# Bias rows stored from 128 partitions, head norms in finer turns, and two preparations moved into the turns of other products

## The reference

```python
# first block: differential attention, then a norm for each head
ob = diff_attention(q1, q2, k1, k2, vh, lam, slopes)
ob = rms_norm(ob, g_subln) * (1.0 - lam_init)
# second block
hm = mlstm_chunkwise(mq, mk, mv, i_gate, log_f)
hm = hm * lax.rsqrt(jnp.mean(hm * hm, axis=-1, keepdims=True) + NORM_EPS)
y_ml = jax.nn.sigmoid(mo) * (hm * mlstm_norm)
x = x + rms_norm_2(jnp.concatenate([y_nsa, y_ml], axis=-1) @ w_out, mix_norm_post)
h = rms_norm_2(x, xattn_norm_pre)
mem_n = rms_norm_2(mem, mem_norm)
q = (h @ w_xq) * XATTN_HEAD_DIM ** -0.5
k, v = jnp.split(mem_n @ w_xkv, 2, axis=-1)
p = jax.nn.softmax(jnp.einsum('bshd,bmhd->bhsm', q, k), axis=-1)
x = x + rms_norm_2(jnp.einsum('bhsm,bmhd->bshd', p, v).reshape(B, S, D_MODEL) @ w_xo, xattn_norm_post)
```

## Time and profile before

| | us |
|---|---|
| median of 3 runs | 2117.9 |
| lowest and highest | 2117.48, 2119.8 |
| the profiled execution | 2119.19 |
| its span in the trace | 2117.4 |
| TensorE busy in the span | 1821.1 |
| DVE busy | 742.0 |
| ACT busy | 641.0 |
| POOL busy | 169.1 |

### The profile page before, as it was taken

How to read it: one execution, slowest core, us unless ns; L and a number is a source line. 1 busy time by engine, 2 the same in 40 slices (tenths; PEclk the granted TensorE clock), 3 DMA queues, 4 the chain that set the end, 5 groups by cost and what they waited for, 6 DMA issues and landing times.

```text
span 2117.4 us, 21821 instructions
## 1 busy us (share of the span) xinstructions
PE 1821.1 (86%) x8908; PEld 1276.2 (60%) x8908; DVE 742.0 (35%) x1540; ACT 641.0 (30%) x1077; POOL 169.1 (8%) x134
## 2 busy tenths in 40 slices
PE   7969999997898887888489777997889879999998
PEld 4848656786333333333167555765678758888887
DVE  4245344455111111211432355544463452222323
ACT  4224455423011000100331245454342342222223
POOL 0000001130111111110000000001000100000111
PEclk9979889998899999989789688997999989999999
DMA  7541100248699999999722110111232112322311
GB/s 210 76 141 65 55 20 21 73 180 310 253 397 417 415 408 398 412 407 411 281 75 84 41 58 18 41 60 69 98 123 80 50 40 96 113 80 80 119 60 40
DMA packets 78434, 337.57 MB, mean 159 GB/s; under 512 B 7883, under 2 KB 15691, under 8 KB 65400
## 3 DMA queue, kind: packets, MB, share of 16 engines
q1 hardware_dynamic: 73208, 327.70, 41.4%
q0 software_dynamic: 5120, 8.40, 1.2%
HBM read 327.69 MB, written 16.78 MB: 163 GB/s over the span
## 4 chain that ended last, share of the span: by engine, by line
PE 48%; DMA 18%; DVE 8%; ACT 5%; issue 2%; POOL 0%; SPq 0%; DVEq 0%; POOLq 0%; ACTq 0%
PE ps L500 47%; DMA otf<-in_w 17%; DVE splitr L565 1%; ACT splitr L576 1%; ACT arenaf L2637 1%; PE ps L2500 1%; ACT hr L771 1%; DVE arenaf L2585 1%; DVE xf L2893 1%; DVE tq L797 0%; DVE hr L805 0%; DMA arenaf<-yd 0%; DVE xf L2099 0%; DVE arenaf L2603 0%; DVE otf L2432 0%
## 5 line engine op out<-in xcount | busy, mean ns | idle before, releaser
L500 PE MATMUL ps<-hr,splitr 128*128 128x512 f32 x2400 | 586.3, 404 | 14.3 <-POOL hr L848 9.8
L500 PEld LDWEIGHTS ps<-hr,splitr 128*128 128x128 f32 x2400 | 464.1, 196 | 116.1 <-POOL hr L848 12.1
L500 PE MATMUL ps<-splitr,hr 128*128 128x512 f32 (+2 forms) x1584 | 291.4, 346 | 28.1 <-ACT arenaf L726 23.1
L500 PEld LDWEIGHTS ps<-splitr,hr 128*128 128x128 f32 x1584 | 253.4, 197 | 62.3 <-ACT arenaf L726 23.3
L565 DVE TENSOR_TENSOR splitr<-ring,splitr 128x2048 fp32r<-128x2048 f32 x63 | 146.8, 2333 | 237.7 <-ACT splitr L576 237.6
L500 PE MATMUL ps<-ring,arenaf 128*64 128x512 f32 x352 | 176.9, 661 | 21.8 <-DMA ring<-in_w 21.8
L576 ACT CAST splitr<-ring 128x2048 fp32r<-128x2048 f32 x63 | 119.7, 1903 | 188.4 <-PE ps L500 162.0
L500 PE MATMUL ps<-arenaf 128*64 128x128 f32 (+11 forms) x898 | 134.8, 364 | 27.2 <-DVE arenaf L1684 8.7
L1848 DVE TENSOR_TENSOR arenaf<-arenaf,ps 64x512 f32<-64x512 f32 x32 | 21.8, 681 | 329.0 <-ACT arenaf L1843 329.0
L565 DVE TENSOR_TENSOR splitr<-arenaf,splitr 128x2048 fp32r<-128x2048 f32 x29 | 69.5, 2396 | 139.7 <-ACT splitr L576 139.7
L1843 ACT ACTIVATE arenaf<-ps 64x512 f32<-64x512 f32 x32 | 19.0, 594 | 326.4 <-PE ps L500 326.4
(11 more groups left out here) (342 smaller groups left out, 2001.7 us busy)
## 6 DMA issues: line engine op xcount, KB each, us to landing
ring<-in_w SPq DMA_DIRECT2D x22, 2048.0 KB, 35.6
arenaf<-in_w SPq DMA_DIRECT2D x22, 2048.0 KB, 40.5
splitf<-in_w SPq DMA_DIRECT2D x21, 2048.0 KB, 35.3
hf<-in_w SPq DMA_DIRECT2D x20, 2048.0 KB, 36.0
ring<-in_w_in SPq DMA_DIRECT2D x11, 2048.0 KB, 10.9
otf<-in_w SPq DMA_DIRECT2D x11, 2048.0 KB, 39.6
ring<-in_w_gate_up SPq DMA_DIRECT2D x6, 2048.0 KB, 7.8
arenaf<-in_w_in SPq DMA_DIRECT2D x4, 2048.0 KB, 21.1
```

The lines of the kernel that those rows point to most:

```text
L500: return te.matmul(out, lhsT, rhs, start=start, stop=stop)
```

## The change

- The biases are repeated 16 times on DVE (`rlx`, 33x128), so TensorE's product gives each row in 16 partitions; `vr` is now 128x1024 in `junk`, and the store writes 8 copies from each of 128 partitions. The waits for the store move from step 5 of the differential attention (DVE and ACT) to DVE's start of fox.
- DVE's part of `spread` becomes a task of its own, `table`, a turn ahead of TensorE's. `ML_SIDE` and `ML_LAST` are laid out anew, with one step of a head norm in a turn.
- `pe_T` and `walk_T` call `tick` for each token tile of each piece. The cross weights get the group of `wout`, so their first piece follows `wout1`'s last.
- In steps 12 to 15 of `xa` the first four rows of outputs are split; behind it the other four.

```diff
-            dense(f"xkv{c}", "w_xkv_2", 512 * c, 512, mode="FFTT"[c], group="x")
+            dense(f"xkv{c}", "w_xkv_2", 512 * c, 512, mode="FFTT"[c], group="m")
...
-            dense(f"xq{c}", "w_xq_2", 512 * c, 512, group="x")
+            dense(f"xq{c}", "w_xq_2", 512 * c, 512, group="m")
...
-        vr = OT[0:8, 1536:2560]
+        vr, rlx = junk[:, 1024:2048], OT[0:33, 1536:1664]
...
-                    if i == 0 and len(names) > 1:
                         tick()
-                for t in range(nt):
-                    tick()
...
                     lead(p)
-                    if i == 0 and len(jobs[job]) > 1:
+                    for t in range(nt):
+                        if i == len(jobs[job]) - 1:
+                            done(t)
                         tick()
-                for t in range(nt):
-                    done(t)
-                    tick()
...
-                elif what == "spread":
+                elif what == "table":
...
-                sp.dma_start(io["vd"], vr.rearrange("h (o n) -> h o n", o=1).broadcast_to([8, 128, 1024])).then_inc(
+                sp.dma_start(io["vd"].rearrange("h (a e) n -> (h a) e n", e=8),
+                             vr.rearrange("p (o n) -> p o n", o=1).broadcast_to([128, 8, 1024])).then_inc(
...
-                    mm(ps[0:8, :], rl, oh[:, 512 * half:512 * half + 512], True, True).then_inc(
+                    mm(ps[:, :], rlx, oh[:, 512 * half:512 * half + 512], True, True).then_inc(
...
                     if t == 2:
+                        for w in ve_at(("rl",)):
+                            ve.wait_ge(*w)
+                        ve.tensor_copy(thirds(rlx, 8), rl.rearrange("p (h o) -> p h o", o=1)
+                                       .broadcast_to([33, 8, 16])).then_inc(*ve_done("biases repeated", ("rlx",)))
                         ve_lead_to(0)
...
-                    if part == "beat" and u == 5:
-                        for w in ve_at(("vd",)):
-                            ve.wait_ge(*w)
...
-            HEADS = [(what, h) for h in range(4) for what in ("square", "mean", "spread", "times")]
+            HEADS = [(what, h) for h in range(4) for what in ("square", "mean", "table", "spread", "times")]
...
-            ML_SIDE = {8: [("square", 0), ("mean", 0)], 9: [("spread", 0)], 10: [("times", 0), ("gate", 0)],
-                       11: [("split", 0)], 12: [("square", 1), ("mean", 1)], 13: [("spread", 1), ("split", 1)],
-                       14: [("times", 1), ("gate", 1)], 15: [("split", 2)], 16: [("square", 2), ("mean", 2)],
-                       17: [("spread", 2), ("split", 3)], 18: [("times", 2), ("gate", 2)]}
-            ML_LAST = [("square", 3), ("mean", 3), ("spread", 3), ("times", 3), ("gate", 3)]
+            ML_SIDE = {8: [("square", 0)], 9: [("mean", 0)], 10: [("table", 0)], 11: [("spread", 0), ("split", 0)],
+                       12: [("times", 0), ("gate", 0), ("square", 1)], 13: [("mean", 1), ("split", 1)],
+                       14: [("table", 1)], 15: [("spread", 1), ("split", 2)],
+                       16: [("times", 1), ("gate", 1), ("square", 2)], 17: [("mean", 2), ("split", 3)],
+                       18: [("table", 2)], 19: [("spread", 2)]}
+            ML_LAST = [("times", 2), ("gate", 2), ("square", 3), ("mean", 3), ("table", 3), ("spread", 3), ("times", 3),
+                       ("gate", 3)]
...
+            XO_EARLY = {12: 0, 13: 1, 14: 2, 15: 3}
...
+                        if u in XO_EARLY:
+                            c = XO_EARLY[u]
+                            for w in se_at(("xout", c // 2, c % 2), ("prod", "xq1", 3)):
+                                se.wait_ge(*w)
+                            se_high(OT3[:, c, :], Hh[:, c, :], "xo", c)
...
-                ve_split8(OT3, Hh, Hl, "xo")
+                for c in (4, 6):
+                    ve_low(OT3[:, c, :], Hh[:, c, :], Hl[:, c, :], "xo", c)
-                se_split8(OT3, Hh, "xo")
+                for c in range(4, 8):
+                    se_high(OT3[:, c, :], Hh[:, c, :], "xo", c)
-                ge_split8(OT3, Hh, Hl, "xo")
+                for c in (1, 3, 5, 7):
+                    ge_low(OT3[:, c, :], Hh[:, c, :], Hl[:, c, :], "xo", c)
```

More of the change, by code:

```diff
@@ L1345, in ve_fox @@
                 beats, tick = beside_fox(ve_lead, no_gate), ticker(HEADS, head)
-                for w in ve_at(*S.ends("diff")):
+                for w in ve_at(*S.ends("diff"), ("vd",)):
                     ve.wait_ge(*w)
@@ L2937, in ve_wout @@
                 tick(True)
-                ve_lead_to(jobs["xkv0"][0])
             def se_wout():
```

15 lines of the change are left out of this document (6 added, 9 removed).

## The result

The changed kernel takes 2058.1 us (median of 4 runs, 2055.6 to 2060.7) against 2117.7 us for the kernel before on the same chip: a ratio of 0.972, with a 95% interval of 0.970 to 0.973. That is 59.6 us less, 5 us beyond the forecast of 2063 us. In the profiled executions the span falls from 2117.4 to 2058.9 us, 58.5 us.

A forecast was written before the change was run, and what follows sets the result against it. TensorE, busy 86% of the span, and its gaps were taken to bound the kernel. Terms +0.3 - 25.3 - 3.5 - 9.0 - 13.9 - 3.6 = -55.0 us gave 2063 us, range 2047 to 2086 us.

The forecast's parts named there:

- The diagnosis: Differential attention: the slow store from 8 partitions delays weights `fq`; a 23.05 us wait and 2.2 us slow clock go, -25.3 us.
- (b): Rival: the store is slow from its many 4 KB copies, not its 8 partitions, so weights stay late; 2088 us, chance 0.07.
- (d): Rival: the store, on all engines but no faster, keeps `fq` back longer; about 2134 us at 130 us, chance 0.03.
- The start: First norm: the added 33x128 copy on VectorE lies on the path ahead of the first projection, +0.3 us.
- Fox: First block's head norms: of 6.6 us waits, 1.6 us saved at one and 1.9 us at the other, -3.5 us.
- mLSTM: Head norms there: 15.1 us of waits within the turns, partly returning as squares come 1.4 us later; -9 us.
- `wout` and the cross weights: Memory's norm and cross weights: 10.49 us wait, 1.2 us clock and 3.2 us tail go, +1 us late weights; -13.9 us.
- the slow clock behind it too: Cross weights: 144 matmuls behind the 10.49 us wait run faster once it goes, 1.2 us.
- Cross attention and `xo`: Outputs' split: the 5.06 us wait before `xo0` goes, early splits cost +1.5 us in the steps; -3.6 us.
- The rule against the change: Cross attention: VectorE and GpSimd share ports under an exclusive lock; GpSimd's two lows could lose 3.2 us instead of 1.5.
- Rival (a): Small waits only move to the next turn; only the store and the 10.49 us wait count; 2081 us, chance 0.19.
- Rival (c): More than counted: all waits named vanish, and the clock with them, -71 us; 2047 us, chance 0.09.

The follow-up runs named there:

- square_first: Changed kernel with mLSTM's spread products in the side products' banks and each next head's square ahead of `times` and `gate` of the head before; 2052.4 us.
- spread_later: As square_first, with one empty turn in fox between `table` and `spread`; 2050.5 us.
- store_undone: Changed kernel with the bias rows stored from 8 partitions again and the waits for the store at step 5 again; 2083.8 us.
- store_behind: Kernel before with its slow store from 8 partitions issued behind the load of the weights `fq` instead of ahead of it; 2092.4 us.
- store_alone: Kernel before with only the new store of the bias rows; 2093.9 us.
- heads_undone: Changed kernel with the head norms' turns as before in fox and mLSTM; 2074.0 us.
- spread_banks: Changed kernel with mLSTM's spread products written to the two banks of the side products; 2057.3 us.
- xo_undone: Changed kernel with all eight splits of the cross attention's outputs behind it again; 2063.9 us.

## Why the prediction was right, point by point

**The diagnosis** (one store keeps `fq` back) held in every part: no wait over 2 us between 95 and 130 us, `fq` at 48.9 us where below 65 was asked. -25.3 was forecast for the stage, -25.4 measured. Nothing else was late, as the working said. Rivals (b) and (d) are gone: the same copies of 4 KB leave at eight times the rate from 128 partitions.

**The start**: +0.3 was forecast, +1.66 measured. The copy itself takes 0.21 us. The stage's length is 78.8 to 81.2 us in the kernels with that copy (`square_first` 78.78, `spread_later` 80.29, after 81.18) and 79.5 to 81.5 in three without it (before 79.52, `store_undone` 79.81, `store_behind` 81.51), so the difference lies within the spread between executions and says nothing of the edit.

**Fox**: -3.5 was forecast as gaps, -7.1 measured. The first term, "there it saves 1.6 us", held: 1.4 us in each comparison at an equal clock, though the two profiled waits (4.12 and 4.26 us) hide it. The step that failed is "at the other [...] most of it, 1.9 us": 2.46 us stood there and 2.17 us stand in fox after it, now for a `times`. Two small waits that the sum did not name, 0.37 us (L931) and 0.78 us (L1373), went instead, so that the gaps fell by some 3 us at an equal clock (9.07 and 9.34 us to 6.1 to 6.2; 10.93 and 10.94 us to 7.75 to 7.79), near the forecast by luck. The rest, some 4 us, is a term that the sum did not have: matmuls behind the first wait that ran at a higher clock.

The stage has a spread of its own: with the finer turns fox took 186.1 to 188.7 us in eight executions, with the old ones 195.7 to 198.2 in four (the kernel before, `store_alone`, `store_behind`, `heads_undone`). So the turns are worth 7 to 12 us there. The three of the eight at 188.6 us are those whose first twelve products ran at full clock. A slow clock ahead of a wait that another engine ends costs nothing; in these three the matmuls behind the wait take 1.0 to 2.6 us longer than in the other five. Why the slow stretch falls now here and now there is open.

**mLSTM**: -9.0 was forecast, -5.3 measured. As gaps it was -7.8, near the forecast; L922 and L927 are together at 6.2 us, below the 9 asked. Two things took from it. The new wait of 3.58 us for `times` is the effect that the working had as "each square comes some 1.4 us later", and it was sized too small; the bank that `spread` holds was not in the forecast, and `spread_banks` shows that without it the time is lost at the square. And TensorE was busy for 2.6 us longer, at a clock of 0.81 in place of 0.85. In the seven executions with this layout (`spread_banks` counted) it was busy for 72.8 to 73.4 us, in three of the four with the old one for 70.8 to 71.0, but in the fourth (`store_behind`) for 75.3 us, at 0.79. So this is not shown to come from the missing gaps.

**`wout` and the cross weights**: -13.9 was forecast, -12.2 measured. The wait of 10.49 us is gone whole. The tail from the last product of `xkv3` to `xq0` is 1539.12 - 1533.03 = 6.1 us, where 6.4 were worked out and 9.6 stood before. The +1 us for late weights did not come: there is a new wait of 1.05 us, but another of 1.36 us has gone, and all waits for L565 in `xkv` come to 3.5 us, before 3.7.

```profile
1479.74 11.67 PE L500 MATMUL ps<-otr,splitr 128*128 128x256 f32 x96
1492.47 5.99 PE L500 MATMUL ps<-otr,splitr 128*128 128x256 f32 x48 [1.05 <-DVE splitr L565]
...
1500.60 7.46 PE L500 MATMUL ps<-otr,splitr 128*128 128x256 f32 x48 [2.15 <-DVE splitr L565]
...
1539.12 23.48 PE L500 MATMUL ps<-hr,splitr 128*128 128x512 f32 x96 [4.78 <-POOL hr L844]
```

The first 144 matmuls take 11.67 + 5.99 = 17.66 us where they took 19.18, and this looks like the 1.2 us of clock that were forecast. But the next 48 take 7.46 us where they took 5.99: over all 192 it is 25.1 us after and 25.2 before. The slow stretch has moved behind another wait, and the step "the slow clock behind it too" gave nothing. A further 1.0 us goes to `xkv2` and `xkv3`: from their first product to the end of their last they take 24.7 us, before 23.8 (waits left out), with five groups of flips between the products instead of three.

The largest part of what is missing lies in `wout`. Without its gap the stage had 58.56 - 10.49 = 48.07 us of work and now has 49.23, with no gap in it. The windows before (up to the gap) and after:

```profile
1467.86:1516.00 48.14, 48.08 (x210) 39.10 (x210) 16.76 (x17) 14.21 (x24) 4.28 (x3) 0.96 0.40 143
```

```profile
1430.51:1479.74 49.23, 49.23 (x210) 39.79 (x211) 22.89 (x24) 19.29 (x31) 5.57 (x4) 0.94 0.39 140
```

It is the clock again, 0.96 and 0.94. The stage takes 48.0 us in `square_first`, `spread_later` and `heads_undone`, and 49.1 to 49.2 us in every kernel with mLSTM as in the change and no gap in `wout`. So the 1.2 us go with the layout of mLSTM ahead of it, not with the turns. A lower clock in a stretch without a gap was on the list of signs of being wrong, and here it came true.

**Cross attention and `xo`**: -3.6 was forecast, -6.8 measured. The gap went as forecast (5.06 us; the stage's gaps fell from 8.19 to 3.55). The +1.5 us for the early splits in the steps was too much: TensorE's waits for cells there are 2.90 and 0.65 us, 0.4 us more than the 2.90 and 0.23 before. And the clock behind the gap was not counted: 2.1 us in `xo`. Over all executions it is 1.5 to 2.1 us: 50.5 to 51.1 us in the four with the gap, 49.0 us in the nine without.

The rule against the change, the exclusive lock between VectorE and GpSimd (the Trainium skill, SBUF — State Buffer, Who interferes with whom), fits one operation of the trace, and cost little. First GpSimd's first early split, then the operation of the softmax that VectorE had at the same moment; then this operation as a whole (ns least, median, most), after the change and in `xo_undone`:

```profile
1615.65 1.27 POOL L985 TENSOR_TENSOR hr<-otf,hr 128x512 fp32r<-128x512 f32 x1 [77.18 <-ACT hr L974]
```

```profile
1615.63 1.45 DVE L3082 TENSOR_SCALAR arenaf<-arenaf,cells 128x256 f32<-128x256 f32 x1
```

```profile
L3082 DVE TENSOR_SCALAR arenaf<-arenaf,cells x16: 353/354/1445, 1569.0 to 1619.4; 128x256 f32<-128x256 f32 x16
```

```profile
L3082 DVE TENSOR_SCALAR arenaf<-arenaf,cells x16: 353/354/356, 1563.5 to 1613.2; 128x256 f32<-128x256 f32 x16
```

One of the sixteen took 1.1 us longer beside GpSimd's 1.27 us, and none did without the early splits. TensorE's waits grew by the 0.4 us above, where the estimate had 3.2: the second of GpSimd's two operations found VectorE nearly idle.

**`xq0`**, -1.3 us, is put down to nothing: with equal code its length falls near 24.3 us or near 25.7 us (`store_alone` 25.76, `spread_later` 25.61, `square_first` 24.20).

**Rival (a)** was right in part for the head norms, where 2.17 and 3.58 us stand at another place for a `times`, and wrong for the rest. **Rival (c)** was not reached by the changed kernel, but 2050.5 us for `spread_later` lies 3.5 us from it, so most of what it named was to be had.

The sum came out 3.5 us short of the span's fall of 58.5 us. Its largest term was right to 0.1 us, but the others missed by up to 3.7 us in both directions: fox by 3.6 and cross attention with `xo` by 3.2 us too little, mLSTM by 3.7, the cross weights with `wout` by 1.7 and the start by 1.4 us too much. Another 3.3 us fell in stages that were put down for nothing and whose lengths differ as much with equal code. That these errors nearly cancel is luck. What the sum lacked in fox, mLSTM, `wout` and `xo` is the clock.

## What to carry to other kernels

When one load is late, look at what was issued ahead of it on the same queue before making anything faster: issuing the needed load first gave the same here as a store eight times faster (ratios 0.988 and 0.989). Price a gap of TensorE with what stands behind it, by the rows of the same matmuls at both levels of the clock (5.06 us cost 6.5 us here), but follow the slow stretch to where it goes: behind one removed gap it only moved to the next wait. Compare a wait before and after only if TensorE came to it at the same clock: 4.12 and 4.26 us hid a gain of 1.4 us. And where a step is moved one turn ahead, read what the engine that makes it has in that turn; if the wait comes back under another name, find the operation that is late rather than the buffer at which it shows.

## What the runs showed of the hardware

- A store from SBUF with a repeated source goes at 51, 205 and 400 GB/s from 8, 64 and 128 partitions, all with copies of 4 KB: 64 partitions reach half of what 128 do.
- A load issued right behind a store of 51 GB/s landed 86.9 us after its issue; behind the same bytes at 205 GB/s after 26.5 us, at 400 GB/s after 17.3 us.
- A VectorE operation of 0.35 us took 1.45 us beside a GpSimd operation of 1.27 us that began 0.02 us after it; in `xo_undone`, without that GpSimd operation there, all sixteen took 0.35 us.
- Twelve matmuls took 4.49 us or 3.03 us ahead of a wait that VectorE ended, and the product behind the wait started 15.2 us into the stage either way.
- With the change the granted clock was lower in mLSTM (0.85 to 0.81) and `wout` (0.96 to 0.94), and higher in fox (0.90 to 0.93), `xo` (0.93 to 1.00) and the differential attention (0.92 to 1.00). With equal code it was 0.85 and 0.79 in mLSTM (`store_alone`, `store_behind`), so part of such a difference is no effect of an edit. What decides between them no run here separates.
